# Running token mixers, merge, routing and expert retrieval of a decoder layer as one interleaved stage

## The reference

```
h = rms_norm(x, norm1_g) * (1 + sc1) + sh1
z = h @ w_in                                 # q, k, v, gates of both mixers
o_a = gla(...)    ; o_a = rms_norm(o_a, gla_gn_g) * silu(ra)
o_b = softmax over three dilated causal windows (128/1, 512/4, 2048/16), 4 heads each
merged = sigmoid(gza) * (o_a @ w_branch_a) + sigmoid(gzb) * (o_b @ w_branch_b)
x = x + g1 * (merged @ w_out)
h2 = rms_norm(x, norm2_g) * (1 + sc2) + sh2
q = h2 @ peer_wq ; s1, s2 = scores of q against 128 + 128 keys, for 8 heads
top 16 of each, top 16 of the 256 sums: 128 experts e and gates per row
x = x + g2 * sum over 128 experts of gate * gelu(h2 . u[e]) * v[e]
y = rms_norm(x, final_g)
```

## Time and profile before

| what | us |
| --- | --- |
| median of three runs (5919.67 to 5924.78) | 5920.66 |
| the profiled execution | 5913.2 |
| its span | 5911.4 |
| PE busy in the span | 4123.8 |
| DVE busy | 3217.2 |
| POOL busy | 1425.6 |
| ACT busy | 755.0 |

### The profile page before, as it was taken

The page is one execution under the profiler, slowest core; times in us unless marked ns, Lnnn a source line. Parts: engine busy times, 40 slices in busy tenths (PEclk is TensorE's granted clock), DMA queues, the critical chain, the costliest instruction groups (busy, mean ns, idle before and its releaser), DMA issues. The chain is left out here.

```text
span 5911.4 us, 32347 instructions
## 1 busy us (share of the span) xinstructions
PE 4123.8 (70%) x9956; PEld 1891.1 (32%) x9956; DVE 3217.2 (54%) x6401; ACT 755.0 (13%) x1542; POOL 1425.6 (24%) x1040
## 2 busy tenths in 40 slices
PE   6999999996777677687782555555555555655566
PEld 1444444443444444333330222222222222212222
DVE  2000000002343444379998777777777777777775
ACT  1000000001222221022210001010101001010101
POOL 0000000000000000000000555555555555555553
PEclk8999999997767767698986777777777777777777
DMA  7134433273010004311101999999999999999996
GB/s 254 52 132 146 152 126 118 91 269 138 32 46 38 33 33 156 143 46 46 39 27 45 422 421 421 421 421 422 412 421 412 422 421 412 422 413 422 408 421 262
DMA packets 246792, 1409.81 MB, mean 238 GB/s; under 512 B 23292, under 2 KB 75172, under 8 KB 109797
## 3 DMA queue, kind: packets, MB, share of 16 engines
q0 software_dynamic: 148896, 1083.11, 44.2%
q1 hardware_dynamic: 73270, 276.73, 13.4%
q10 hardware_dynamic: 24512, 48.68, 2.1%
HBM read 1341.66 MB, written 159.08 MB: 254 GB/s over the span
## 5 line engine op out<-in xcount | busy, mean ns | idle before, releaser
L1545 PE MATMUL ex_out<-ex_UV,ex_diag 128*128 128x512 f32 x2048 | 1480.3, 890 | 1139.9 <-ACT ex_diag L1581 1139.9
L1526 POOL DMA_INDIRECT ex_UV<-in_peer_uv,expert_idx x1024 | 1401.9, 1369 | 3043.6 <-POOLq L139 1854.6
L1636 DVE CUSTOM_DVE_ANT_0 ex_UV<-ex_UV,ex_h 128x1024 f32<-128x1024 f32 x1024 | 1231.0, 1222 | 436.3 <-DMA ex_UV<-in_peer_uv,expert_idx 436.3
L1545 PEld LDWEIGHTS ex_out<-ex_UV,ex_diag 128*128 128x128 f32 x2048 | 566.5, 290 | 2053.0 <-ACT ex_diag L1581 1269.3
L390 PE MATMUL z_ps<-win,hT 128*128 128x464 f32 x3024 | 1189.2, 555 | 16.3 <-ACT z_stage L372 11.1
L390 PEld LDWEIGHTS z_ps<-win,hT 128*128 128x128 f32 x3024 | 539.3, 179 | 665.4 <-issue 649.3
L720 DVE TENSOR_SCALAR mx_xb<-mx_O,mx_ab 128x128 f32<-128x128 f32 x32 | 9.0, 344 | 1236.1 <-PE mx_O L533 1236.1
L1652 DVE SCALAR_TENSOR_TENSOR ex_acc<-ex_UV,ex_w,ex_acc 128x1024 f32<-128x1024 f32 x504 | 647.6, 1285 | 19.0 <-DVE ex_w L1599 1.2
L1574 ACT ACTIVATE ex_th<-ex_arg 128x4 f32<-128x4 f32 x256 | 52.6, 205 | 2209.7 <-DVE ex_arg L1593 2209.7
L466 POOL DMA_DIRECT2D mx_masks<-table_masks x1 | 0.7, 713 | 1365.9 <-POOLq L139 1365.9
L372 ACT COPY z_stage<-z_ps 128x464 f32<-128x464 f32 x189 | 102.8, 545 | 1103.0 <-PE z_ps L390 1077.6
(11 more groups left out here) (319 smaller groups left out, 3401.1 us busy)
## 6 DMA issues: line engine op xcount, KB each, us to landing
out_kv_w_sample<-in_cache_kv_w SPq DMA_DIRECT2D x8, 8188.0 KB, 41.6
win<-in_w_in SPq DMA_DIRECT2D x21, 1856.0 KB, 10.0
z_scratch<-z_stage ACTq DMA_DIRECT2D x21, 1856.0 KB
ada<-in_ada_w SPq DMA_DIRECT2D x12, 2048.0 KB, 7.9
ex_UV<-in_peer_uv,expert_idx POOLq DMA_INDIRECT x1024, 19.2
out_kv_w_sample<-in_cache_kv_w SPq DMA_DIRECT2D x8, 2044.0 KB, 16.8
mx_zg<-z_scratch SPq DMA_DIRECT2D x8, 1544.0 KB, 6.9
mx_zq<-z_scratch SPq DMA_DIRECT2D x8, 1536.0 KB, 9.9
```

The lines of the kernel that those rows point to most:

```text
L1526: pool.indirect_dma_start(out=UV[slot % RING][:, :], out_offset=None, in_=uv, in_offset=bass.IndirectOffsetOnAxis(ap=index, axis=0)).then_ ...
L1545: last = nc.tensor.matmul(out[:, b, :], diag[:, n % DIAGS, :], value(slot)[:, b * 512:(b + 1) * 512], start=(slot == mine[0]), stop=(slot ...
L1636: nc.vector.tensor_tensor_reduce(out=half(slot), in0=half(slot), in1=h2[i % 2][:, :], scale=1.0, scalar=0.0, op0=ALU.mult, op1=ALU.add, ac ...
```

## The change

Stages 2, 4 and 5 become one, `mix_and_experts` (L739 of the changed file), which runs after `sample_mixers`. It goes through nine windows. In window w the 128 expert slots of tile w - 1 run (none in window 0), and between them the "front" of tile w: mixers, merge and routing (in window 8 merge and routing of the sample rows). Each engine's front is a generator that yields the slot number ("tick") at which its next piece may come:

```diff
+def until(lane, tick):
+    while lane[0] is not None and lane[1] <= tick:
+        try:
+            lane[1] = next(lane[0])
+        except StopIteration:
+            lane[0] = None
...
+                for win in range(TILES + 1):
+                    lane = [front(win), -1]
+                    for c in range(SLOTS if win else 0):
+                        slot = (win - 1) * SLOTS + c
+                        pe.wait_ge(s["dots"], slot + 1)
+                        until(lane, c)
+                        if c >= GRP and on_pe(slot - GRP):
+                            add_value(slot - GRP)
+                    until(lane, END)
```

```diff
-RING = 12
-DIAGS = 4
+RING = 10
+DIAGS = 8
+LATE = 92
...
-    return slot >= PROMPT_SLOTS or slot % 2 == 1
+    return slot >= PROMPT_SLOTS or slot % 2 == 1 or slot % SLOTS >= LATE
```

```diff
+                def load_keys(i, h):
+                    b, at = h % 2, 0
+                    for g, j0, n in key_spans(i):
+                        sp.dma_start(keys[b][:, at:at + n * P], k.kT[g * AH + h, :, j0 * P:(j0 + n) * P]).then_inc(kvl[b], 16)
+                        sp.dma_start(vals[b][:, at:at + n * P], k.vS[g * AH + h, :, j0 * HD:(j0 + n) * HD]).then_inc(kvl[b], 16)
+                        at += n * P
+                def load_weights(i, n):
+                    u = 8 * i + n
+                    at_least(sp, s["product"], u - 1)
+                    sp.dma_start(wr[u % 2][:, 0:MW[n + 1] - MW[n]], k.i["merge_w"][:, MW[n]:MW[n + 1]]).then_inc(wl[u % 2], 16)
```

Sigmoid and silu are computed with Tanh, without reciprocals:

```diff
-                    link(nc.vector.reciprocal(er[:, :], er[:, :]))
...
+                    dve.wait_ge(s["gz_tanh"], i + 1)
+                    dve.wait_ge(s["product"], 8 * i + 2)
+                    nc.vector.scalar_tensor_tensor(out=gz[0:R, 0:D], in0=gz[0:R, 0:D], scalar=1.0, in1=bigf[0:R, 0:D], op0=ALU.add, op1=ALU.mult).then_inc(s["mg_steps"], 1)
```

More of the change, by code:

```diff
@@ new lines, in key_tiles, with turn_blocks, blocks_of, blocks_upto @@
+def key_tiles(i):
+    return sum(n for _, _, n in key_spans(i))
+def turn_blocks(i):
+    return -(-key_tiles(i) // 4)
+def blocks_of(i, h, parity):
+    per = lambda n: (turn_blocks(n) + 1 - parity) // 2
+    return sum(4 * per(n) for n in range(i)) + h * per(i)
+def blocks_upto(i, h):
+    return blocks_of(i, h, 0) + blocks_of(i, h, 1)
+def score_pieces(i):
+    out, at = [], 0
+    for g, j0, n in key_spans(i):
+        mask = MASK0[g] + AHEAD[g] - (n - 1) * P
+        done = 0
+        while done < n * P:
+            w = min(n * P - done, 512 - at % 512)
+            out.append((g, at, mask + done, w))
+            at, done = at + w, done + w
+    return out
@@ L1466, in experts @@
+    wl = [k.sem(f"fx_w_loaded{b}") for b in range(2)]
+    kvl = [k.sem(f"fx_keys_loaded{b}") for b in range(2)]
+    loaded = [k.sem(f"fx_expert_loaded{b}") for b in range(RING)]
     uv = k.i["peer_uv"]
@@ new lines, in front, with add_value @@
+                def front(i):
+                    if i < TILES:
+                        yield from mix(i)
+                    yield from merge(i)
+                def add_value(slot):
+                    i, n = slot // SLOTS, pe_upto[slot]
+                    if n == pe_upto[i * SLOTS]:
+                        at_least(pe, s["out"], 3 * i - 2)
+                    pe.wait_ge(s["diag"], n + 1)
+                    for b in range(2):
+                        last = nc.tensor.matmul(out[:, b, :], diag[:, n % DIAGS, :], value(slot)[:, b * 512:(b + 1) * 512],
+                                                start=(n == pe_upto[i * SLOTS]), stop=(n + 1 == pe_upto[i * SLOTS + SLOTS]))
+                    last.then_inc(s["pe_slots"], 1)
@@ new lines, in front, with tail_square, tail_root @@
+                def front(i):
+                    if i < TILES:
+                        yield from mix(i)
+                    yield from merge(i)
+                def tail_square(i, R, junk):
+                    act.wait_ge(s["out"], 3 * i + 3)
+                    nc.scalar.activation(junk, y[0:R, :], ACT.Square, accum_out=rs[0:R, 0:1]).then_inc(s["esq"], 1)
+                def tail_root(i, R):
+                    act.wait_ge(s["evar"], 2 * i + 2)
+                    nc.scalar.activation(rs[0:R, 1:2], rs[0:R, 0:1], ACT.Sqrt).then_inc(s["eroot"], 1)
@@ new lines, in front, with gains @@
+                def front(i):
+                    if i < TILES:
+                        yield from mix(i)
+                    yield from merge(i)
+                def gains(rows, norm, count_, name, before):
+                    dve.wait_ge(s[name], count_)
+                    nc.vector.tensor_scalar(mods[rows, 0, :], mods[rows, 0, :], 0.5, None, ALU.mult).then_inc(s["gains"], 1)
+                    nc.vector.scalar_tensor_tensor(out=mods[rows, 2, :], in0=mods[rows, 2, :], scalar=1.0, in1=norm[rows, :], op0=ALU.add, op1=ALU.mult).then_inc(s["gains"], 1)
+                    dve.wait_ge(s["gains"], before + 2)
@@ L1661, in _ @@
                 dve.wait_ge(s["dots"], PROMPT_SLOTS + NS)
[L1662 to L1666 removed]
+                gelu_argument(PROMPT_SLOTS // GRP, aS, cubeS, argS, agS, gT[:, :])
```

1603 lines of the change are left out of this document (775 added, 828 removed).

## The result

| | before | after |
| --- | --- | --- |
| median of four runs, us | 5921.26 | 5364.01 |
| lowest to highest | 5919.67 to 5924.78 | 5360.92 to 5370.55 |
| span of the profiled execution | 5911.4 | 5365.0 |
| PE, DVE busy in the span | 4123.8, 3217.2 | 3953.5, 2782.3 |

The ratio of the times is 0.9062, with a 95% interval of 0.9051 to 0.9073: 9.4% less time. The forecast was 5350 us.

The account below looks back on a forecast made before the run. Experts were bound by DMA transfers, while mixers and merge/routing left DMA 85% idle. Interleaved: 1366 + 152 + 3 + 238 + 7 x 447 + 387 + 72 = 5347, given as 5350 us; range 4930 to 5720.

Parts of the forecast that it names:

- four stretches: A window's ticks 0-27, 28-60, 61-92 and 93-127, each costed as its fullest resource plus waits: 447 us; chance 0.68.
- window 0: First window, with no experts to hide behind: 238 us; over 300 would show the forecast wrong.
- Rival 1: Transfers hide everything, PE and DVE catch up: window 393 us, total 4944 us; chance 0.15.
- rival 2: PE becomes the bound at its low clock: window 480 us, total 5591 us; chance 0.10.
- rival 3: Nothing overlaps, each front step costs its old length: window 545 us, total 6033 us; chance 0.07.
- Linear attention: Ticks 0 to 27: DVE's 83 us of work plus 27 of waits, 110 us; ends 83 and 137.
- half as much again: Ticks 0 to 27: DVE's old 18.5 us of waits grow to 27, as answers also stand behind PE's two slots.
- costed at nothing: Among the items given no time: the key store that must land before the next loads.
- Heads: Ticks 28 to 60, four heads: DVE's 80 us plus 6 of waits per head, 104 us; ends 98 and 134.
- Merge: Ticks 61 to 92: bound by DMA, gathers 81 us plus weights 35.6 plus 4, 121 us; ends 110 and 150.
- Routing: Ticks 93 to 127: DVE's 101 us of work and 10 of score waits, 111 us.
- The last window and the end: Last window, with only the 8 sample rows' merge, 387 us; the end with sample slots and no lookahead, 72 us.

Follow-up runs that it names:

- key_store: Changed kernel with the turned gated keys and the silu's Tanh written to other places, so ACT doesn't wait for the key store: 5327.9 us, 0.8988.
- mid_dve: Changed kernel with the values of slots 56 to 87 all on DVE, so no ring buffer waits for PE in the merge ticks: 5366.9 us, 0.9050.
- dve_merge: Changed kernel with 13.1 us more DVE work (two reciprocals) at tick 69 of tiles 1 to 7: 5377.6 us, 0.9089.
- dve_routing: Changed kernel with 13.1 us more DVE work (two reciprocals) at tick 93, ahead of the routing, in tiles 1 to 7: 5439.5 us, 0.9184.
- no_key_stream: Changed kernel with attention keys and values not loaded (16 columns each), the resident final gain read instead: 5326.1 us, 0.9003.

## Why the prediction was right

**The mechanism.** A window as four stretches, each with its own limit, came out at 447.1 us for a forecast of 447, and each of the seven (427 to 470) lies within the 412 to 480 that I gave; window 0 took 258, under the 300. Rival 1 (transfers hide everything, 393) falls with the DVE and PE waits of each window; rival 2 (PE the bound) with PE busy 316 of 462 us in window 6; rival 3 (no overlap, 545 or more) by the measured 427 to 470. The DMA share over a window was 0.90 to 0.94 (forecast 0.88), and DVE's waits for PE were 33 to 60 us a window (forecast 30 to 60). Two signs of the prediction served badly. The share was highest in the merge ticks only in window 6, in windows 1 to 5 it was higher in the heads and in window 7 in the routing ticks. And POOL waited 240 to 290 us a window for buffers, more than the 150 that I gave as a sign of rival 3, with the transfers at 0.90 and more.

**Term by term.** That the mean window was met to within 0.1 us is luck: the linear attention was 8 us shorter than forecast and the merge 12 longer, and the two nearly cancel.

- *Linear attention, 110 forecast, 102.1 measured.* DVE's work, 83 in the sum, is 79 (window 1, without a tail, 74). The rest of the stretch, forecast at 27, is 17 to 19 us in the windows without the wait for the key store, about the old stage's 18.5, and 27 to 29 with it. So "half as much again" for PE's slots failed: the waits are no longer than the old ones. What brought four windows to nearly the forecast length is the store that I "costed at nothing", and there only as a wait of the next loads, where it is ACT's copy that waits; `key_store` shows that it costs 36 us in all. Window 3, without that wait, to be held against window 6 above:

```profile
2648.20:2744.30 96.10, 58.52 (x159) 27.26 (x157) 79.09 (x147) 23.13 (x54) 35.90 (x28) 0.79 0.90 348
```

- *Heads, 104 and 103.8.* The mean is right, but the range of 92 to 117 over the windows grows with the key tiles, and most of what grows is DVE's wait for late scores (4.5 us in window 1, 25 in windows 6 and 7), not the bytes' share: without the streamed keys they still range from 88 to 107. Of the 14 us that I took for the key traffic only 6.3 come back when it goes.
- *Merge, 121 and 132.7.* This is the term that was mis-sized. Transfers are a bound of it, as said: 13 us of DVE are almost free there, and the weights are worth 19 us a window. But I took the gathers' and weights' bytes at the full 412 GB/s. They went at 376 to 392, so the 50.7 MB that were moved took 133 us and not 123; with the ring unburdened of PE the rate was 398 to 413. And I put nothing behind the transfers but DVE's 74 us of work: the front's chain, that work with its waits for products and Tanh in order, leaves 113.6 us when the weights are gone, so 19 of their 35.6 us came back.
- *Routing, 111 and 108.4.* Bound by DVE: 96.7 busy, and 10.5 of 13.1 added us appear in the stretch.
- *Window 0.* From the barrier at 1523 to the first dot at 1780.7 it took 258, not 238. The start was 23 instead of 16, the merge 83 instead of the 62 of PE's work: PE was busy 55 us of it, and 16.7 of the rest it waited for streamed weights, which the sum of window 0 had left out:

```profile
PE fr_big L1065 <- DMA fr_arena<-in_merge_w: 16.7, 3, 7.6
```

- *The last window and the end.* 394 for 387, and 61 for 72.

So 1780.7 + 7 x 447.1 + 394.1 + 60.6 = 5365, the span, against 1759 + 3129 + 387 + 72 = 5347 in the sum.

**The bandwidth limit.** By the 358 GB/s of the Trainium skill ("DMA: Bandwidth & Descriptors", section "Where 436 GB/s comes from") a window would have taken an estimated 453 us. That lies close to the measured mean, but not for this reason, and the trace disagrees with it: 393 to 411 GB/s were moved in the heads of windows 1 to 4, and 398 to 413 in the merge ticks of `mid_dve`. Row for one of them:

```profile
1873.47:1965.35 91.88, 56.59 (x172) 29.18 (x172) 71.46 (x136) 12.18 (x36) 43.55 (x34) 0.85 1.01 411
```

**Left open.** How deep a ring would pay, since no run has more than ten buffers. And why the waits for the key store come in windows 2, 5, 6 and 7 and not in 1, 3 and 4: they aren't tied to the window, since long first ticks (106 us and more, with that wait) stand in windows 5 and 6 of `dve_merge`, 4 and 5 of `dve_routing`, and 2 and 6 of `no_key_stream`.

## What to carry to other kernels

When two stages are interleaved, cost each stretch of the interleaved order by itself, as its fullest resource plus the waits that one engine's order exposes, and not the stage by its mean load. Put a known piece of work into each stretch to learn what an engine's time is worth there; here the same 13 us cost 2 us in one place and 10 in another. On an engine that serves both streams, what matters is who stands behind its answer: bundling values to release buffers earlier lost 110 us, because DVE, with all its dots queued behind, then waited longer for the other stream's answer.

## What was not expected of the hardware

The granted clock of PE was 0.50, its lower level of 1.2 GHz, through the first 104 us of window 0, after a stretch in which PE was busy 113 of 157 us at 0.64; it rose to 0.80 in the merge, with PE busy 55 of 83 us. In window 6 it was 0.73 in the linear attention, 0.85 in the heads, 0.82 in the merge and 0.92 in the routing ticks. PE's busy share, 0.63, 0.68, 0.73 and 0.69 there, doesn't give that order; its longest wait, 11.8, 10.0, 10.2 and 5.8 us, does in this one window. No run here tests what sets it.
